# Differential attention and its gated product in one unrolled block, with each head's scores directly behind its v projection

## The chip, the cores and the metric

The kernel runs on one core of a Trainium2 chip. The metric is device time in microseconds (us), from one execution's start to its end; three executions of the kernel before were timed, and one further execution was profiled. TensorE (PE), VectorE (DVE), ScalarE (ACT), GpSimd (POOL) and SyncE (SP, which issues the DMA) each run their own instructions strictly in the order written, and wait for one another through semaphores.

## What is computed

Two transformer layers in fp32 for 512 tokens and model width 1024. The change is in the second layer, in the differential attention branch and its gate:

```python
h = _rmsnorm(x, mix_pre_g)
q, k, v, z, xbc, dt_raw, gate_logits = jnp.split(h @ w_in, cuts, axis=-1)
p = probs(q1b, k1) - lam * probs(q2b, k2)          # causal softmax, two maps a head, 8 heads
o = _rmsnorm(p @ v, da_subln_g, SUBLN_EPS) * (1.0 - lam_init)
attn_out = o @ w_branch_attn
dt = jax.nn.softplus(dt_raw + ssd_dt_bias)         # cumulative sums of -exp(A_log) * dt feed the SSD branch
g_attn, g_ssd = jnp.split(jax.nn.sigmoid(gate_logits + b_gate), N_BRANCH, axis=-1)
mixed = (g_attn * attn_out + g_ssd * ssd_out) @ w_mix_out
```

The kernel keeps activations transposed (features on partitions, tokens in the free dimension). Heads are 128 wide, so one head's q, k or v is one tile of 128 features by 512 tokens.

## The kernel before

Everything that is a matrix product with weights is done in **units**. A unit is a 128x1024 piece of weights that SP loads into one of two raw buffers (`c.raw`); ACT rounds it to `w_hi` (L155, `split_hi`), DVE subtracts to get `w_lo` (L166, `split_lo`), and PE then issues 24 matmuls of 128x512 (L193 to L195, `multiply_tile`) into one of two PSUM banks (`acc`). Buffers alternate by the unit's number, so unit k+2 is split into the buffers that unit k leaves. `split_hi(k)` therefore waits until PE has used unit k, and `split_lo(k)` for that `split_hi`. An accumulator bank is free again when its reader has taken it (`acc_free`), and the tile two later may start.

The attention is `da_stage`. For each of 8 heads PE runs the units q, k and v; ACT copies the three tiles out of the banks (L1842). A head further has: `turn_v` (v to token-major by four transposes into the bank `mixed`, L1805); `scores` (two maps by four row blocks of 128, 256, 384 and 512 columns, in two banks in turn, L1273); `maxima` (DVE reads each score tile out of its bank with the mask added and the row maximum, L1287, which frees the bank for the tile after next); `exponentials` (ACT, eight of them, L1299); `weights` (DVE: reciprocal and the difference of the two maps, L1909 to L1922); `transposes` of the probabilities on PE (L1308), each block taken out by ACT (`take_transposes`, L1316) from one of two banks; `outputs` (L1327); and the norm of the output: square (ACT L1851), its sum over the features by a matmul with ones (`mixed`, L1830), root (ACT L1855 and L1857), product (DVE L1927), and the hi/lo split (ACT L1861, DVE L1932).

A head's second half (transposes, outputs, norm) is done one head later, among the units of the next head. PE's order in one head is q unit, `turn_v` of the head one back, k unit, `transposes` of the head one back, `scores` of this head, `outputs` of the head one back, v unit, sum of squares of the head one back. The loop over heads is a device loop (`Fori`) of three rounds with two heads each; the first head and the last are written out.

Then come a barrier, a block in which GpSimd clears the semaphores (`clear_semaphores`, L247), and `gated_stage`: eight rounds of one gate unit (`h` times the gate's weights, sigmoid on ACT, L1694) and one value unit (the attention's output times `w_branch_attn`), whose product DVE forms (L1726) straight from the bank. Between its rounds it runs the small steps of the SSD branch (`SsdSteps`): `project` (24 matmuls), `argument`, `exponentials`, `logarithm`, `steps` (a chain of DVE operations on 32x512 up to a scan, L2204 to L2212), `turn` (transposes of the sums), `tables`. The next stage, `ssd_stage`, begins behind another barrier.

## Time and profile before

| | |
|---|---|
| median of 3 executions | 2933.54 us (2932.46 to 2940.70) |
| the profiled execution: its own time | 2936.5 us |
| its span, first to last instruction | 2934.5 us |
| PE busy | 2687.7 us, 92% of the span |
| DVE, ACT busy | 1291.6 us (44%), 1051.4 us (36%) |
| mean granted PE clock | 0.958 of 2.4 GHz |

How to read it: the span is what the instructions cover; the execution's own time is 2.0 us longer. A matmul's busy time is modelled and overlaps its neighbours, so positions in time are taken from the starts of rows: the distance from the start of a piece of PE work to the start of the next piece is what the piece costs on PE. A row of the timeline is a start, a duration, the engine, the line, what is written and read, and a count; in brackets stand the idle time in front of it and who ended that. A row of busy time by stretch gives start and end, its length, then busy time and count of PE, of PE's weight loads, of DVE, ACT and POOL, the granted PE clock (1.00 is 2.4 GHz, 0.50 is 1.2 GHz), the DMA share and GB/s.

### The profile page before, as it was taken

Reading aid. Unit: us, or ns where it says so; the run is one execution under the profiler, and the core shown is the slowest. Engines: PE = TensorE matmul, PEld = TensorE weight load, DVE = VectorE, ACT = ScalarE, POOL = GpSimd, SP = SyncE. Lnnn points to the kernel's source line nnn. Section 1 sums busy time; section 2 is a strip of 40 time slices with the busy share of each in tenths; the row PEclk is TensorE's granted clock in tenths of the full one; section 3 lists DMA queues with packets and bytes.
Section 4 is the critical chain, followed back from the end, with each engine's and each line's share of the span. In section 5 each row is a group of like instructions: output and inputs, shape, how many; then the busy total and the mean of one; then the engine's idle time right before and its main releaser. Section 6 shows DMA issues by size and latency. Waiting matters only on the chain. (4 is left out here: it accounts for less than half of the span.)

```text
span 2934.5 us, 34310 instructions
## 1 busy us (share of the span) xinstructions
PE 2687.7 (92%) x12052; PEld 2161.0 (74%) x12052; DVE 1291.6 (44%) x1765; ACT 1051.4 (36%) x1661; POOL 180.4 (6%) x111
## 2 busy tenths in 40 slices
PE   4998999999999999996999898988799798799997
PEld 3777777788888888884676677766677587588885
DVE  5343544344443444424343236666634633533333
ACT  4343544243222323223344334444522433323221
POOL 0000000010001000012000000011202300100000
PEclk8999999999999999997898899999999899899998
DMA  2212121222223323331111122232122131122232
GB/s 88 66 64 74 59 70 60 91 93 93 100 91 99 97 95 98 97 94 51 58 50 50 63 92 96 82 107 93 64 93 100 65 101 65 58 94 99 94 97 81
DMA packets 69457, 241.00 MB, mean 82 GB/s; under 512 B 7968, under 2 KB 8992, under 8 KB 69264
## 3 DMA queue, kind: packets, MB, share of 16 engines
q1 hardware_dynamic: 69392, 240.14, 25.2%
q8 instruction: 40, 0.66, 0.1%
q14 instruction: 25, 0.20, 0.0%
HBM read 237.94 MB, written 2.16 MB: 82 GB/s over the span
## 5 line engine op out<-in xcount | busy, mean ns | idle before, releaser
L193 PE MATMUL acc<-h_hi,w_hi 128*128 128x512 f32 x2176 | 873.8, 402 | 47.7 <-PEq L227 18.5
L166 DVE TENSOR_TENSOR w_lo<-w_raw,w_hi 128x1024 fp32r<-128x1024 f32 (+1 forms) x422 | 513.9, 1218 | 824.2 <-ACT w_hi L155 823.6
L194 PE MATMUL acc<-h_lo,w_hi 128*128 128x512 f32 x2176 | 854.7, 393 | 0.0
L195 PE MATMUL acc<-h_hi,w_lo 128*128 128x512 f32 x2176 | 854.3, 393 | 0.0
L155 ACT ACTIVATE w_hi<-w_raw 128x1024 fp32r<-128x1024 f32 (+1 forms) x422 | 441.5, 1046 | 1138.1 <-PE acc L195 1135.8
L193 PEld LDWEIGHTS acc<-h_hi,w_hi 128*128 128x128 f32 x2176 | 413.5, 190 | 148.3 <-issue 58.5
L194 PEld LDWEIGHTS acc<-h_lo,w_hi 128*128 128x128 f32 x2176 | 413.5, 190 | 90.4 <-issue 6.4
L195 PEld LDWEIGHTS acc<-h_hi,w_lo 128*128 128x128 f32 x2176 | 413.0, 190 | 87.8
L193 PE MATMUL acc<-9_hid_hi,w_hi 128*128 128x512 f32 x352 | 136.9, 389 | 0.0
L194 PE MATMUL acc<-9_hid_lo,w_hi 128*128 128x512 f32 x352 | 136.9, 389 | 0.0
L195 PE MATMUL acc<-9_hid_hi,w_lo 128*128 128x512 f32 x352 | 136.9, 389 | 0.0
L613 POOL TENSOR_TENSOR ssq<-ssq,10_sq 128x512 f32<-128x512 f32 x24 | 42.4, 1766 | 1275.7 <-ACT 10_sq L602 1275.7
L756 DVE TENSOR_TENSOR 9_up<-acc,10_rstd 128x512 f32<-128x512 f32 x44 | 30.4, 691 | 128.7 <-PE acc L195 128.7
L751 DVE TENSOR_TENSOR 9_gate<-acc,10_rstd 128x512 f32<-128x512 f32 x44 | 30.4, 691 | 105.8 <-PE acc L195 96.0
L194 PEld LDWEIGHTS acc<-9_hid_lo,w_hi 128*128 128x128 f32 x352 | 66.1, 188 | 13.8
L195 PEld LDWEIGHTS acc<-9_hid_hi,w_lo 128*128 128x128 f32 x352 | 66.1, 188 | 13.7
L193 PEld LDWEIGHTS acc<-9_hid_hi,w_hi 128*128 128x128 f32 x352 | 66.1, 188 | 13.7
L193 PE MATMUL acc<-29_hid_hi,w_hi 128*128 128x512 f32 x176 | 68.5, 389 | 0.0
L194 PE MATMUL acc<-29_hid_lo,w_hi 128*128 128x512 f32 x176 | 68.5, 389 | 0.0
L195 PE MATMUL acc<-29_hid_hi,w_lo 128*128 128x512 f32 x176 | 68.5, 389 | 0.0
L193 PE MATMUL acc<-merged_hi,w_hi 128*128 128x512 f32 x128 | 52.2, 407 | 11.8 <-PEq L227 6.1
L2490 POOL TENSOR_TENSOR 17_xs<-17_xs,17_moved 128x384 f32<-128x384 f32 x16 | 18.5, 1155 | 683.6 <-DVE 17_xs L2473 683.0
(427 smaller groups left out, 3438.2 us busy)
## 6 DMA issues: line engine op xcount, KB each, us to landing
w_raw<-in_w_gu SPq DMA_DIRECT2D x132, 512.0 KB, 3.4
w_raw<-in_w_down SPq DMA_DIRECT2D x48, 512.0 KB, 3.5
w_raw<-in_w_ssd SPq DMA_DIRECT2D x40, 512.0 KB, 3.4
w_raw<-in_w_swa SPq DMA_DIRECT2D x28, 512.0 KB, 3.4
w_raw<-in_w_gla SPq DMA_DIRECT2D x24, 512.0 KB, 3.4
w_raw<-in_w_da SPq DMA_DIRECT2D x24, 512.0 KB, 3.4
w_raw<-in_w_ssd_out SPq DMA_DIRECT2D x24, 512.0 KB, 3.4
w_raw<-in_w_xa SPq DMA_DIRECT2D x24, 512.0 KB, 3.4
```

The source lines that it names most:

```text
L155: c.nc.scalar.activation(c.w_hi[:, k % 2, 0:chunks * P], c.raw[:, k % 2, 0:chunks * P], ACT.Copy).then_inc(c.hi_done, 1)
L166: c.nc.vector.tensor_tensor(c.w_lo[:, k % 2, 0:chunks * P], c.raw[:, k % 2, 0:chunks * P], c.w_hi[:, k % 2, 0:chunks * P].bitcast(F32), AL ...
L193: pe.matmul(out, hi, x_hi[:, j, 0:cols], start=first, stop=False)
L194: pe.matmul(out, hi, x_lo[:, j, 0:cols], start=False, stop=False)
L195: mm = pe.matmul(out, lo, x_hi[:, j, 0:cols], start=False, stop=final)
L613: pool.tensor_tensor(self.c.ssq[:], self.c.ssq[:], self.sq[:, par, :], ALU.add).then_inc(self.summed, 1)
L751: dve.tensor_tensor(gate[:], c.acc[0][:], root.rstd[:], ALU.mult).then_inc(gate_done, 1)
L756: dve.tensor_tensor(up[:], c.acc[1][:], root.rstd[:], ALU.mult).then_inc(c.acc_free[1], 1)
L2490: pool.tensor_tensor(y[:, j, P:], y[:, j, P:], moved[:, j % 2, P:], ALU.add).then_inc(q["joined"], 1)
```

## The change

`da_stage` and the attention's `gated_stage` become one stage, `branch_stage`, with no device loop. All 40 units stand in one list: for heads 0 to 5 q, k, v and the gate unit with the head's number; for heads 6 and 7 q, k and v; then gate units 6 and 7 and the eight value units. On PE a head's `scores` stand behind its v unit, and `outputs` and the sum of squares of the head one back directly behind the scores, ahead of the gate unit. ACT and DVE get orders of their own, written out: ACT splits the k unit's weights ahead of `take_transposes`, and writes each gate's sigmoid straight into the result buffer `part_attn`, with a load of the sigmoid's table ahead and of the exponential's table behind. DVE splits the weights for q, k and v and then runs `maxima`. The steps of the SSD branch stand at fixed places: `project` and `transposes` of head 7 between gate units 6 and 7, `turn` behind value unit 3, the last matmul (`last_rows`) behind value unit 4. They take the banks and buffers of scores, q and k, which are idle by then. `clear_semaphores` runs ahead of this block and once more ahead of the last feed-forward, instead of in the middle. The number of matmuls is the same.

```diff
--- before.py
+++ after.py
@@ class Norm
-        self.rstd, self.normed = sb("rstd", [P, S]), sb("normed", [P, NORM_BUFS, S])
+        if places is None:
+            normed = sb("normed", [P, NORM_BUFS, S])
+            places = [normed[:, n, :] for n in range(NORM_BUFS)]
...
@@ gated_stage
-        rounds_with(pe, body, *([None, steps.project, None, steps.turn] if steps else []))
+        rounds_of(c, pe, body)
...
@@ class SsdSteps
-        self.proj, self.turned, self.whole = ps("proj"), [ps("turned0"), ps("turned1")], ps("whole")
+        self.proj, *self.turned, self.whole = banks
...
+    def last_rows(self, pe):
+        H = SSD_HEADS
         pe.wait_ge(self.tok_done, 1)
         pe.matmul(self.whole[:, 0:NT * H], self.last[:], self.by_tok[:], start=True, stop=True).then_inc(self.whole_done, 1)
@@ new
+def branch_units(a):
+    order = [(n, g) for g in range(DA_HEADS - 2) for n in ("q", "k", "v", "gate")]
+    order += [(n, g) for g in (DA_HEADS - 2, DA_HEADS - 1) for n in ("q", "k", "v")]
+    order += [("gate", DA_HEADS - 2), ("gate", DA_HEADS - 1)] + [("value", g) for g in range(KC)]
...
+@stage
+def branch_stage(c, ctx, places, y_hi, y_lo, causal, gain, part, steps):
...
+    @block.sync
+    def _(sp):
+        sp.dma_start(mask[:], causal).then_inc(tables_in, 16)
+        steps.load(sp)
+        n = c.stream.n
+        for k in range(n):
+            ahead, u = (c.stream, k + 2) if k + 2 < n else (c.following, k + 2 - n)
+            chunks, src = ahead.units[u]
+            if k == places["value", KC - 2]:
+                steps.store(sp)
+            sp.wait_ge(c.lo_done, c.unit + k + 1)
+            load_unit(c, sp, k % 2, chunks, src(0))
+        sp.wait_ge(steps.stored, 16)
...
+        def turn_v(g):
+            wait_evacuated(c, pe, 0, places["v", g])
+            pe.wait_ge(mixed_free, 2 * g + 1)
+            for n in range(NT):
+                mm = pe.transpose(mixed[:, n * P:(n + 1) * P], v[:, g % 2, n * P:(n + 1) * P], c.ident[:])
+            mm.then_inc(v_turned, 1)
...
+        def mean_square(g):
+            pe.wait_ge(squared, g + 1)
+            pe.wait_ge(mixed_free, 2 * g + 2)
+            pe.matmul(mixed[:], c.ones[:], sq[:], start=True, stop=True).then_inc(total, 1)
...
+        unit(0, "q")
+        unit(0, "k")
+        unit(0, "v")
+        score(0)
+        unit(0, "gate")
+        turn_v(0)
+        for g in range(1, H):
+            unit(g, "q")
+            unit(g, "k")
+            att.transposes(pe, g - 1, (g - 1) % 2)
+            unit(g, "v")
+            score(g)
+            outputs(g - 1)
+            mean_square(g - 1)
+            if g not in LATE:
+                unit(g, "gate")
+            if g < H - 1:
+                turn_v(g)
+        unit(H - 2, "gate")
+        turn_v(H - 1)
+        pe.wait_ge(att.read, H * att.n + 2)
+        steps.project(pe)
+        att.transposes(pe, H - 1, (H - 1) % 2)
+        unit(H - 1, "gate")
+        outputs(H - 1)
+        mean_square(H - 1)
+        for j in range(4):
+            value(j)
+        pe.wait_ge(att.pt_done, att.turns + H * NT)
+        steps.turn(pe)
+        value(4)
+        steps.last_rows(pe)
+        for j in range(5, KC):
+            value(j)
...
+        def square(g):
+            act.wait_ge(att.outs, g + 2)
+            act.activation(sq[:], att.out[0][:], ACT.Square).then_inc(squared, 1)
...
+        def gate(g):
+            k = places["gate", g]
+            weights_hi(g, "gate")
+            act.preload_act_table(ACT.Sigmoid)
+            bias = c.small[:, SMALL["b_gate_2"][0] + g:SMALL["b_gate_2"][0] + g + 1]
+            act.activation(part[:, g, :], c.acc[k % 2][:], ACT.Sigmoid, bias=bias).then_inc(c.acc_free[k % 2], 1)
+            act.preload_act_table_set(EXP_LN_SET)
...
+        for g in range(H):
+            take(g, "q", q)
+            weights_hi(g, "q")
+            take(g, "k", k_)
+            weights_hi(g, "k")
+            if g > 0:
+                att.take_transposes(act, g - 1)
+            take(g, "v", v)
+            weights_hi(g, "v")
+            if g > 0:
+                square(g - 1)
+            att.exponentials(act, g, g % 2)
+            if g > 0:
+                roots(g - 1)
+                y_split(g - 1)
+            if g == 4:
+                steps.split_weights(act)
+            if g not in LATE:
+                gate(g)
+            if g < H - 1:
+                take_v_tok(g)
+        gate(H - 2)
+        take_v_tok(H - 1)
+        steps.exponentials(act)
+        att.take_transposes(act, H - 1)
+        gate(H - 1)
+        square(H - 1)
+        roots(H - 1)
+        y_split(H - 1)
+        for j in range(2):
+            weights_hi(j, "value")
+        steps.logarithm(act)
+        for j in range(2, 5):
+            weights_hi(j, "value")
+        steps.tables(act)
+        for j in range(5, KC):
+            weights_hi(j, "value")
...
+        def product(j):
+            k = places["value", j]
+            wait_evacuated(c, dve, 0, places["gate", j])
+            wait_tile(c, dve, 0, k)
+            dve.tensor_tensor(part[:, j, :], part[:, j, :], c.acc[k % 2][:], ALU.mult).then_inc(c.acc_free[k % 2], 1)
+            weights_lo(j, "value")
+        for g in range(H):
+            weights_lo(g, "q")
+            weights_lo(g, "k")
+            weights_lo(g, "v")
+            att.maxima(dve, g, g % 2)
+            if g == H - 2:
+                weights(g)
+            if g > 0:
+                normed_output(g - 1)
+            if g == 4:
+                steps.split_weights_lo(dve)
+            if g not in LATE:
+                weights_lo(g, "gate")
+            if g == H - 1:
+                y_split(g - 1)
+                weights_lo(H - 2, "gate")
+            if g != H - 2:
+                weights(g)
+            if 0 < g < H - 1:
+                y_split(g - 1)
+        steps.argument(dve)
+        weights_lo(H - 1, "gate")
+        normed_output(H - 1)
+        y_split(H - 1)
+        for j in range(2):
+            product(j)
+        steps.steps(dve)
+        for j in range(2, 5):
+            product(j)
+        steps.to_end(dve)
+        for j in range(5, KC):
+            product(j)
@@ build_program
         with ExitStack() as f:
...
+        clear_semaphores(c)
...
-                da_stage(c, s_da, s_att, *y_da, a["causal"], "mix_pre_g_2")
-                clear_semaphores(c)
-                gated_stage(c, s_att, s_ssd, [[y_da]], 1, None, None, None, part, 0,
-                            (tok, scratch, a["w_dt"], a["keep"], a["last"]))
+                branch_stage(c, s_da, s_ssd, branch_places, *y_da, a["causal"], "mix_pre_g_2", part,
+                             (tok, scratch, a["w_dt"], a["keep"], a["last"]))
...
+        clear_semaphores(c)
         with ExitStack() as f:
```

In the order of instructions, on DVE in the scores of the first head: the last weight split before the scores' reads, and what follows (`w_lo` is a unit's low part, `13_score` the two score banks, `12_mask` the causal mask, `13_s` the scores in SBUF; ISA rows on a score are the reads of `maxima`). The kernel before:

```order
L166 TENSOR_TENSOR w_lo<-w_raw,w_hi 128x1024
L1287 ISA 13_s_0,13_top<-13_score,12_mask 128x128
L1287 ISA 13_top 128x1
L1287 ISA 13_s_1,13_top<-13_score,12_mask 128x128
L1287 ISA 13_top 128x1
```

The change:

```order
L166 TENSOR_TENSOR w_lo<-w_raw,w_hi 128x1024 x3
L1291 ISA 13_s_0,13_top<-13_score,12_mask 128x128
L1291 ISA 13_top 128x1
L1291 ISA 13_s_1,13_top<-13_score,12_mask 128x128
L1291 ISA 13_top 128x1
```

Before, one weight split (that of q's slot) stands ahead of the reads and the others behind; now all three (q, k, v) stand ahead, in every head.

On ACT, around the k unit of a head with a head behind it (`12_k` is k, `13_turn` the banks of the transposed probabilities, `13_pt` their copy, `13_out` the output's bank). The kernel before:

```order
L1842 ACTIVATE 12_k<-acc 128x512
L1314 ISA
L1316 ACTIVATE 13_pt<-13_turn 128x128
L1314 REGISTER_ALU
L1316 ACTIVATE 13_pt<-13_turn 128x256
L1314 REGISTER_ALU
L1316 ACTIVATE 13_pt<-13_turn 128x384
L1314 REGISTER_ALU
L1316 ACTIVATE 13_pt<-13_turn 128x512
L154 ISA
L155 ACTIVATE w_hi<-w_raw 128x1024
```

The change:

```order
L2145 ACTIVATE 12_k<-acc 128x512
L155 ACTIVATE w_hi<-w_raw 128x1024
L1320 ACTIVATE 13_pt<-13_turn 128x128
L1320 ACTIVATE 13_pt<-13_turn 128x256
L1320 ACTIVATE 13_pt<-13_turn 128x384
L1320 ACTIVATE 13_pt<-13_turn 128x512
L2145 ACTIVATE 12_v<-acc 128x512
L155 ACTIVATE w_hi<-w_raw 128x1024
L2155 ACTIVATE 12_sq<-13_out 128x512
```

The weight split of k's slot has moved from behind the four copies of transposed probabilities to ahead of them.

On PE, behind the scores of a head (`12_mixed` with `12_sq` is the sum of squares). The kernel before:

```order
L1273 MATMUL 13_score<-12_k,12_q 128x512
L1321 ISA
L1327 MATMUL 13_out<-13_pt,12_v_tok 128x128 x10
L186 REGISTER_ALU
L193 MATMUL acc<-h_hi,w_hi 128x512
```

The change:

```order
L1277 MATMUL 13_score<-12_k,12_q 128x512 x2
L1331 MATMUL 13_out<-13_pt,12_v_tok 128x128 x10
L2097 MATMUL 12_mixed<-12_sq,ones 128x512
L193 MATMUL acc<-h_hi,w_hi 128x512
```

Before, the v unit's 24 matmuls stood between the outputs and the sum of squares; now nothing does, and the gate unit follows the sum.

## Rows read from the trace of the kernel before

**Rows 1.** Busy time by stretch: head 6, the seam, the gated stage twice

```profile
1569.50:1600.20 30.70, 28.63 (x126) 22.00 (x125) 12.34 (x33) 13.51 (x31) 0.00 (x0) 0.89 0.16 49
1624.60:1646.90 22.30, 9.42 (x39) 6.89 (x37) 7.29 (x14) 8.65 (x15) 0.00 (x0) 0.68 0.00 0
1646.90:1693.50 46.60, 46.56 (x192) 38.31 (x193) 11.60 (x11) 11.47 (x13) 0.00 (x0) 0.93 0.35 115
1693.50:1731.60 38.10, 38.10 (x169) 31.35 (x167) 15.12 (x15) 15.32 (x17) 0.00 (x0) 1.00 0.21 70
```

**Rows 2.** Timeline of PE in one steady head, most of the weight units left out

```profile
1544.67 0.49 PE L1308 MATMUL 13_turn<-ident,13_s 128*128 128x128 f32 x3
...
1546.66 0.49 PE L1273 MATMUL 13_score<-12_k,12_q 64*128 64x128 f32 x4
...
1553.27 4.54 PE L1327 MATMUL 13_out<-13_pt,12_v_tok 128*128 128x128 f32 x20
...
1557.56 0.49 PE L193 MATMUL acc<-h_hi,w_hi 128*128 128x512 f32 x1
...
1563.14 1.02 PE L1830 MATMUL 12_mixed<-12_sq,ones 128*128 128x512 f32 x2
...
1564.24 0.39 PE L194 MATMUL acc<-h_lo,w_hi 128*128 128x512 f32 x1
```

**Rows 3.** Timeline of ACT in the same head

```profile
1540.70 1.06 ACT L155 ACTIVATE w_hi<-w_raw 128x1024 fp32r<-128x1024 f32 x1
1544.87 0.60 ACT L1842 ACTIVATE 12_k<-acc 128x512 f32<-128x512 f32 x1 [3.11 <-PE acc L195]
1545.36 0.55 ACT L1316 ACTIVATE 13_pt<-13_turn 128x128 f32<-128x128 f32 x2
...
1557.85 0.60 ACT L1851 ACTIVATE 12_sq<-13_out 128x512 f32<-128x512 f32 x1 [9.54 <-PE 13_out L1327]
1558.34 0.39 ACT L1299 ACTIVATE 13_s<-13_s,13_ntop 128x128 f32<-128x128 f32 x1
```

**Rows 4.** Timeline of DVE in the same head

```profile
1541.79 1.23 DVE L166 TENSOR_TENSOR w_lo<-w_raw,w_hi 128x1024 fp32r<-128x1024 f32 x1 [2.42 <-ACT w_hi L155]
1547.34 0.29 DVE L1287 CUSTOM_DVE_ANT_0 13_s<-13_score,12_mask 128x128 f32<-128x128 f32 x1 [4.32 <-PE 13_score L1273]
...
1562.84 0.20 DVE L1909 RECIPROCAL 13_rec<-13_den 128x8 f32<-128x8 f32 x1 [7.12 <-ACT 13_s L1299]
...
1566.54 1.23 DVE L166 TENSOR_TENSOR w_lo<-w_raw,w_hi 128x1024 fp32r<-128x1024 f32 x1
1567.68 0.74 DVE L1927 SCALAR_TENSOR_TENSOR 12_y<-13_out,small,12_rstd 128x512 f32<-128x512 f32 x1
```

**Rows 5.** Busy time by stretch: scores and outputs; behind the turn's pause

```profile
1427.90:1434.70 6.80, 6.39 (x22) 4.89 (x23) 3.47 (x10) 0.00 (x0) 0.00 (x0) 0.50 0.07 11
1734.90:1747.60 12.70, 12.70 (x49) 9.99 (x48) 3.06 (x4) 3.63 (x7) 0.00 (x0) 0.87 0.27 89
```

**Rows 6.** Timeline of PE at the seam and at the gated stage's end

```profile
1624.56 1.02 PE L1830 MATMUL 12_mixed<-12_sq,ones 128*128 128x512 f32 x2
...
1639.96 1.13 PE L1830 MATMUL 12_mixed<-12_sq,ones 128*128 128x512 f32 x2 [0.69 <-ACT 12_sq L1851]
1646.94 0.79 PE L193 MATMUL acc<-h_hi,w_hi 128*128 128x512 f32 x1 [5.86 <-PEq L247]
...
1751.53 0.49 PE L193 MATMUL acc<-h_hi,w_hi 128*128 128x512 f32 x1 [3.93 <-PEq L227]
```

**Rows 7.** Timeline of ACT behind a table load

```profile
1725.31 1.28 ACT L1705 ACT_TABLE_LOAD   x1
1726.61 1.06 ACT L155 ACTIVATE w_hi<-w_raw 128x1024 fp32r<-128x1024 f32 x1
```

**Rows 8.** Timeline of DVE: start and end of the chain of SSD steps

```profile
1724.21 0.41 DVE L2204 TENSOR_SCALAR 16_u<-16_e 32x512 f32<-32x512 f32 x1 [0.39 <-DVEq L1738]
...
1733.48 2.36 DVE L166 TENSOR_TENSOR w_lo<-w_raw,w_hi 128x1024 fp32r<-128x1024 f32 x2
```

More of the change, by code:

```diff
@@ L356, in on_vector @@
                     dve.wait_ge(self.lo_done[last % 2], last // 2 + 1)
-                dve.scalar_tensor_tensor(self.normed[:, k % NORM_BUFS, :], self.c.x[:, k, :], vec(self.c, self.gain, k),
+                dve.scalar_tensor_tensor(self.places[k % NORM_BUFS], self.c.x[:, k, :], vec(self.c, self.gain, k),
                                          self.rstd[:], ALU.mult, ALU.mult).then_inc(self.normed_done, 1)
@@ L1623, in gated_stage @@
 @stage
-def gated_stage(c, ctx, branches, per, prior, out_hi, out_lo, out, gate_bias=None, steps=None, whole=None):
+def gated_stage(c, ctx, branches, per, prior, out_hi, out_lo, out, gate_bias=None, whole=None):
     sb, ps, sem = local(c, ctx)
@@ L1633, in gated_stage @@
     units = [1 + len(parts) for parts in branches]
-    steps = SsdSteps(c, ctx, *steps) if steps else None
     block = ctx.enter_context(c.nc.Block())
     split = Split(c, ctx, *whole) if whole is not None else None
-    def rounds_with(eng, body, *beside):
-        if steps is None:
-            return rounds_of(c, eng, body)
-        n = c.stream.rounds
-        cuts = (0, n // 4, n // 2, 3 * n // 4, n - 1)
-        for part, (first, end) in zip(beside, zip(cuts, cuts[1:])):
-            with eng.Fori(first, end) as i:
-                body(i, False)
-            if part is not None:
-                part(eng)
-        body(n - 1, c.following is None)
     def tiles():
@@ L1661, in _ @@
     def _(sp):
-        if steps is not None:
-            steps.load(sp)
         stream_loads(c, sp, c.stream, c.following)
-        if steps is not None:
-            steps.store(sp)
     @block.gpsimd
@@ L1700, in body @@
                                    ACT.Copy).then_inc(hi_done, 1)
-        def then_sigmoid(part):
-            def run(act):
-                part(act)
-                act.preload_act_table(ACT.Sigmoid)
-            return run
-        rounds_with(act, body, *([steps.split_weights, then_sigmoid(steps.exponentials), then_sigmoid(steps.logarithm),
-                                  then_sigmoid(steps.tables)] if steps else []))
+        rounds_of(c, act, body)
     @block.vector
@@ L1745, in body @@
                         dve.wait_ge(lo_done, per * i + t + 1)
[L1746 removed]
+        rounds_of(c, dve, body)
 LAM_INIT = 0.2
[L1753 to L1946 removed]
@@ L2099, with __init__ @@
 class SsdSteps:
-    def __init__(self, c, ctx, tok, scratch, w_dt, keep_in, last_in):
+    def __init__(self, c, ctx, tok, scratch, w_dt, keep_in, last_in, banks, places):
         H = SSD_HEADS
@@ L2160, in exponentials @@
         act.wait_ge(self.dve_done, 1)
-        act.activation(self.e[:], self.x[:], ACT.Abs).then_inc(self.act_done, 1)
+        act.activation(self.e, self.x, ACT.Abs).then_inc(self.act_done, 1)
         act.wait_ge(self.act_done, 2)
-        act.activation(self.e[:], self.e[:], ACT.Exp, scale=-1.0).then_inc(self.act_done, 1)
+        act.activation(self.e, self.e, ACT.Exp, scale=-1.0).then_inc(self.act_done, 1)
     def logarithm(self, act):
@@ L2167, in logarithm @@
         act.wait_ge(self.dve_done, 2)
-        act.activation(self.v[:], self.u[:], ACT.Ln).then_inc(self.act_done, 1)
+        act.activation(self.v, self.u, ACT.Ln).then_inc(self.act_done, 1)
     def tables(self, act):
@@ L2209, in steps @@
         self._step(dve, dve.tensor_tensor(v, v, e, ALU.add))
-        self._step(dve, dve.scalar_tensor_tensor(self.dt[:], self.x[:], 0.0, v, ALU.max, ALU.add))
+        self._step(dve, dve.scalar_tensor_tensor(self.dt[:], self.x, 0.0, v, ALU.max, ALU.add))
         self._step(dve, dve.tensor_scalar(u, self.dt[:], self.a_neg[:], -1.0, ALU.mult, ALU.mult))
@@ L2217, in to_end, with source @@
                                           self.tok[:, :, SUM], ALU.subtract))
+def branch_units(a):
+    order = [(n, g) for g in range(DA_HEADS - 2) for n in ("q", "k", "v", "gate")]
+    order += [(n, g) for g in (DA_HEADS - 2, DA_HEADS - 1) for n in ("q", "k", "v")]
+    order += [("gate", DA_HEADS - 2), ("gate", DA_HEADS - 1)] + [("value", g) for g in range(KC)]
+    def source(n, g):
+        if n in ("gate", "value"):
+            return a["w_attn_2"][g, 0 if n == "gate" else 1]
+        return a["w_da"][g // 2, 3 * (g % 2) + ("q", "k", "v").index(n)]
+    return ([(KC, lambda i, n=n, g=g: source(n, g)) for n, g in order],
+            {u: k for k, u in enumerate(order)})
@@ L2521, in build_program @@
     s_dn2 = down("w_down1_2")
-    s_da = Stream(DA_HEADS // 2, [whole("w_da", u) for u in range(6)], 6)
-    s_att = Stream(KC, [whole("w_attn_2", u) for u in range(2)], 2)
+    units, branch_places = branch_units(a)
+    s_da = Stream(1, units, len(units))
     s_ssd = Stream(SSD_GROUPS, [whole("w_ssd", u) for u in range(10)], 10)
```

300 lines of the change are left out of this document (124 added, 176 removed).

## The prediction

> **What bounds the kernel now.** PE is busy for 92% of the span, so I read PE's row first and ask where it stands still or runs at half clock. I compared stretches of the two stages that the change joins. In the gated stage there is nothing to gain inside the rounds: PE is busy for 46.56 of 46.60 us and 38.10 of 38.10 us [rows 1]. One unit of 24 matmuls costs 24/168 of 38.1, which is 5.44 us. A steady head takes 30.7 us [rows 1] for three units (16.3 us) and 14.4 us of attention work. The seam between the stages takes 22.3 us with PE busy for 9.42, at 0.68 of the clock [rows 1]; exactly, from the sum of squares at 1624.56 to the first gate matmul at 1646.94, 22.4 us [rows 6]. That seam is what the joined block can give back.
>
> Then I looked at how a head's pieces hand over, since the change rewrites these handovers in every head. The timeline of PE shows scores from 1546.66 to 1553.27, outputs to 1557.56, then the v unit to 1563.14, and the sum of squares with no pause before it [rows 2]. Scores are paced by DVE: two banks, and DVE's first read starts 0.68 us after the first score matmul [rows 2, 4]. The square is done long before PE wants it, since the v unit lies between. In a score phase the granted clock falls: 6.8 us at 0.50 in a head, over the last scores and the outputs [rows 5]; at 6.39 busy that costs some 3.2 us a head already.
>
> **The change, priced.** Let T be the end of a head's v unit on PE.
>
> (a) Scores wait for v's weight split. DVE now has all three splits ahead of `maxima`, and the third hangs on v. The first two scores fill both banks at once; then PE stands until DVE reads. From T: ACT starts its copy 0.20 later (as 1544.67 to 1544.87), the next ACT row starts 0.49 later (1544.87 to 1545.36), the low part on DVE starts 1.09 behind the start of the high part (1540.70 to 1541.79), and the next DVE row 1.14 behind that (1566.54 to 1567.68) [rows 2, 3, 4]. Sum 2.92 us, against 0.68 now: 2.24 us. From the first read on, the scores take as long as before (1547.34 to 1553.27, 5.93 us). Queued behind it on PE are outputs and the gate unit; nothing else covers it. Eight heads: +17.9.
>
> (b) Transposes wait for k's weight split. Only two banks take them, so PE stops after the second block until ACT copies. That copy stands 0.69 us behind the k unit now (0.20 and 0.49) and has one split more ahead of it, about 1.0 us (a row of 1.06, [rows 3]). PE had no slack there. Seven heads: +7.0. The last head's is in (f).
>
> (c) The sum of squares waits for the square. The square starts 0.29 us behind the outputs (1557.56 to 1557.85), takes 0.60 and hands over in some 0.05; the same handover showed an idle 0.69 at the seam [rows 2, 3, 6]. 0.94 us in each of seven heads: +6.6.
>
> (d) Head 6 has no gate unit. `turn_v` needs the bank `mixed`, which is free when ACT has read the sum of squares, and ACT does that only behind the eight exponentials of this head. From the end of the outputs: 0.29 + 0.49 for the square, 4.50 for exponentials (1558.34 to 1562.84), 0.72 for the logarithm: 6.0 us. PE is there after 0.94 + 0.87 (the sum of squares, 1563.14 to 1564.24 less one matmul of 0.23), 1.8 us [rows 2, 3, 4]. A stall of 4.2 us. In heads 1 to 5 the gate unit's 5.44 us cover it, with 1.2 us to spare. Behind such a pause the clock is low for a while: 48 weight matmuls took 12.6 of the 12.70 us at 0.87 instead of 10.9, 1.7 us [rows 5]. Together +5.9.
>
> (e) With the pause in front, part of the 6.8 us of low clock now lies in idle time, and the outputs (4.29 us at half clock, half of that at full) run partly fast. Between 0 and 2.1 us; no row tells where the low stretch will begin, so I take 0.8 in seven heads: -5.6.
>
> (f) The tail. Before, beyond its units: the seam 22.4, then 46.6 for 192 matmuls that need 43.5, so 3.1 lost to the low clock, then 3.3 for the turn (1731.60 to 1734.90) and 1.7 for the clock behind it: 30.4 us [rows 1, 5, 6]. Now: `turn_v` 0.4. Transposes of head 7 need ACT, which stands in the SSD exponentials behind `project` (argument, two activations and handovers, then the copies): 4.5 from `project` to the next unit. Then gate unit 7; behind it ACT does a split, two table loads of 1.3 (1725.31 to 1726.61, [rows 7]) and the sigmoid, 4.4 in all, before the square, then 0.65 and the sum of squares 0.87: 5.9. The DVE chain of 9.3 us (1724.21 to 1733.48, [rows 8]) starts 2.5 behind value unit 1, as now beside the split; three units of 16.3 cover it but the split for value unit 4 waits: 2.5 with the turn. `last_rows` needs ACT behind a split and a table load: 3.3. Three pauses with 1.7 of low clock each: 5.1. Sum 21.7, so -8.7.
>
> (g) A clear of the semaphores more than before outside the seam, twice. With one, PE idled 5.86, at the next stage end without one 3.93 [rows 6]: at most 1.9 each, at least nothing. I take 1.0: +2.0 in all.
>
> Costed at nothing: the gates' extra table loads in heads 0 to 5. ACT has the sigmoid done some 11.4 us behind the outputs, and the bank is wanted for the next k unit at 12.9; if that cover were gone, each 1 us late would cost 1 us in six heads. SP's three loads for the SSD steps now stand before the weight stream; the queue's next weights are wanted a unit (5.44 us) later. The weight loads and matmuls are the same in number. The branches of the device loop go, but over the loop turns in the gated stage PE idles for 0.04 us [rows 1], so nothing comes back.
>
> The Trainium skill speaks here: "ScalarE: Activation LUTs", What ACT_TABLE_LOAD costs, gives about 1.28 us for the load and another 1.38 us of drain for every switch. The trace shows the load at 1.28 us and the next row 1.30 us after its start, so no drain [rows 7]. By the page, six loads on the tail's path would add 8.3 us, and the sum would be 33 instead of 25.
>
> **Sum:** 17.9 + 7.0 + 6.6 + 5.9 - 5.6 - 8.7 + 2.0 = +25.1 us. On the profiled execution's own 2936.5 that is 2961.6. That execution stood 3.0 above the median, so around the median 2933.5 the same sum gives 2958.6. I write 2958.
>
> **Rivals.**
>
> 1. The clock falls further. PE idles in a second place of each head (0.94 at the square) and longer at the scores; if a second stretch like that of 6.8 us [rows 5] follows, over the gate unit, seven heads pay 3.2 more, and (e) vanishes: +25 + 22 + 6 = +53 at the worst, 2987; half of that, 2972, if it comes in some heads. For it: at the turn a pause of about 2 us was enough for a low stretch. Against: the heads now recover under one weight unit. The Trainium skill ("TensorE: Matmul & The Clock Gate", A second HAM failure mode) says that frequent short idle times between groups make the clock swing; the trace agrees for the scores.
>
> 2. The joined tail gives nothing: each of its handovers costs what the old seam cost, -8.7 becomes 0, 2967. For it: five waits on ACT in it. Against: PE has units of work between them.
>
> 3. Not slower, by the clock. If the new pause takes in the whole low stretch, each head is 3.2 us better, instead of 0.8 in seven (-16.8 more, and -3.2 in head 0), and the low clock behind the four pauses of (d) and (f) is gone (-6.8): 25.1 - 26.8 = -1.7, 2932. It decides from about 2.2 us a head. Against: the pause lies ahead of the last scores, and a low stretch has so far begun behind low activity, not in it.
>
> 4. The wait behind v does not come, since DVE is served otherwise than I read: (a) falls away, +7.2, 2941: no change that can be told. Against: DVE's row of instructions allows nothing else. Faster than before would need (b) or (c) to be hidden too: 25.1 - 17.9 - 7.0 - 6.6 = -6.4, still within the bound.
>
> **Chances.** Forecast 0.55; rival 1 0.15; rival 2 0.12; rival 3 0.07; rival 4 0.06; something outside these that makes it faster 0.05. What a measurement can tell from no change is 0.3%, 8.8 us. Slower by more: 0.82. Within: 0.12. Faster: 0.06. The range reaches from rival 4's 2941 to some low clock more, 2976. The forecast's own is 2949 to 2970: (e) between 0 and 2.1 a head, (g) between 0 and 3.9.
>
> **What would show it.** In the profile after: two score matmul pairs behind each v unit, then PE idle for about 2.3 us released by DVE's score reads; first DVE read 2.9 us behind the v unit; transposes idle 1.6 instead of 0.6; about 0.7 idle, released by the square, before each sum of squares; one idle of about 4 us before `turn_v` of head 6; a steady head with gate near 39.5 us against 30.7 + 5.4. The prediction is wrong if a head with its gate comes at or under 36.2 us, if no idle time stands at the scores' second pair, or if the tail, from the sum of squares behind head 7's scores to the end of the last value unit, takes less than 75 us or over 90 us (ten units and `project` are 59.9 of it).

## The result, and the profile after

| | before | after |
|---|---|---|
| median | 2933.72 us (2932.46 to 2940.70, 4 runs) | 2972.81 us (2970.03 to 2977.89, 4 runs) |
| ratio to before, 95% interval | | 1.0131 [1.0116, 1.0145] |
| profiled execution, its span | 2936.5, 2934.5 us | 2970.79, 2969.0 us |
| mean granted PE clock | 0.958 | 0.954 |

The changed kernel is 1.3% slower, 39 us by the medians and 34.3 us between the two profiled executions. The forecast was 2958: right in sign, inside the range of 2940 to 2976, but 15 us too low, and the time lies above the forecast's own 2949 to 2970.

PE's timeline of the kernel after, from the scores of head 4 to the first unit of the stage that follows, weight units left out (start, duration, what, and in brackets the idle time in front and who ended it):

```profile
1560.43 0.49 PE L1277 MATMUL 13_score<-12_k,12_q 64*128 64x128 f32 x4
1563.60 1.43 PE L1277 MATMUL 13_score<-12_k,12_q 64*128 64x256 f32 x4 [2.68 <-DVE 13_top L1291]
1565.49 1.99 PE L1277 MATMUL 13_score<-12_k,12_q 64*128 64x384 f32 x4 [0.46 <-DVE 13_top L1291]
1567.95 2.55 PE L1277 MATMUL 13_score<-12_k,12_q 64*128 64x512 f32 x4 [0.46 <-DVE 13_top L1291]
1570.43 4.12 PE L1331 MATMUL 13_out<-13_pt,12_v_tok 128*128 128x128 f32 x20
1575.23 1.12 PE L2097 MATMUL 12_mixed<-12_sq,ones 128*128 128x512 f32 x2 [0.69 <-ACT 12_sq L2155]
...
1657.20 1.12 PE L2097 MATMUL 12_mixed<-12_sq,ones 128*128 128x512 f32 x2 [0.69 <-ACT 12_sq L2155]
1662.21 0.74 PE L2082 MATMUL 12_mixed<-ident,12_v 128*128 128x128 f32 x4 [3.89 <-ACT 12_rstd L2159]
1662.60 0.78 PE L193 MATMUL acc<-h_hi,w_hi 128*128 128x512 f32 x1
...
1675.19 0.49 PE L1312 MATMUL 13_turn<-ident,13_s 128*128 128x128 f32 x3
1677.24 0.96 PE L1312 MATMUL 13_turn<-ident,13_s 128*128 128x128 f32 x7 [1.56 <-ACT 13_pt L1320]
...
1698.26 1.13 PE L2097 MATMUL 12_mixed<-12_sq,ones 128*128 128x512 f32 x2 [0.69 <-ACT 12_sq L2155]
...
1713.34 1.30 PE L1312 MATMUL 13_turn<-ident,13_s 128*128 128x128 f32 x7 [2.10 <-ACT 13_pt L1320]
...
1726.45 1.13 PE L2097 MATMUL 12_mixed<-12_sq,ones 128*128 128x512 f32 x2 [2.82 <-ACT 12_sq L2155]
...
1753.48 0.47 PE L193 MATMUL acc<-y_da_hi,w_hi 128*128 128x512 f32 x1 [1.20 <-DVE w_lo L166]
...
1763.53 0.49 PE L1934 MATMUL 13_turn<-15_by_tok,15_last 128*128 128x128 f32 x2 [2.74 <-ACT 15_by_tok L1958]
...
1781.62 0.39 PE L195 MATMUL acc<-y_da_hi,w_lo 128*128 128x512 f32 x1
1785.01 0.49 PE L193 MATMUL acc<-h_hi,w_hi 128*128 128x512 f32 x1 [3.01 <-PEq L227]
```

The kernel before, from the transposes to the second score pair of the same head:

```profile
1515.08 0.95 PE L1308 MATMUL 13_turn<-ident,13_s 128*128 128x128 f32 x7 [0.62 <-ACT 13_pt L1316]
1515.96 0.49 PE L1273 MATMUL 13_score<-12_k,12_q 64*128 64x128 f32 x4
1516.99 0.93 PE L1273 MATMUL 13_score<-12_k,12_q 64*128 64x256 f32 x4 [0.54 <-DVE 13_top L1287]
```

Every pause that the prediction named is there: 2.68 us before the second score pair, 1.56 in the transposes, 0.69 before each sum of squares, 3.89 before `turn_v` of head 6. The last row stood at 1751.53 before [rows 6], so 33.5 of the 34.5 us of span have come by the end of the joined block; 0.4 of them stand ahead of its first unit (1383.27 before, 1383.66 after).

DVE's timeline at the same scores says who is late:

```profile
1562.11 1.23 DVE L166 TENSOR_TENSOR w_lo<-w_raw,w_hi 128x1024 fp32r<-128x1024 f32 x1 [7.09 <-ACT w_hi L155]
1563.25 0.28 DVE L1291 CUSTOM_DVE_ANT_0 13_s<-13_score,12_mask 128x128 f32<-128x128 f32 x1
```

DVE had been idle for 7.09 us, waiting for v's high part, before it could split and then read the first scores, which had been in their bank since about 1560.9. DVE is 44% busy in this kernel, yet its order alone holds PE up.

One thing the prediction had wrong shows in the durations. The same score pairs took 0.93 and 1.25 us before; in this head the 256-column pair takes 1.43 and the 384-column pair 1.99. The busy time by stretch gives the granted clock (the last number but two), first for the whole head, then around the scores:

```profile
1541.00:1582.00 41.00, 35.15 (x150) 26.48 (x149) 13.45 (x33) 17.67 (x36) 0.00 (x0) 0.88 0.16 52
1563.40:1564.40 1.00, 0.80 (x4) 0.71 (x4) 0.35 (x4) 0.00 (x0) 0.00 (x0) 0.60 0.16 33
1564.40:1573.40 9.00, 8.07 (x25) 4.79 (x23) 3.31 (x13) 0.00 (x0) 0.00 (x0) 0.50 0.17 55
1573.40:1574.40 1.00, 1.00 (x8) 0.95 (x7) 0.00 (x0) 0.00 (x0) 0.00 (x0) 0.78 0.00 0
```

The clock stands at its lower level, 1.2 GHz, from just behind the pause almost to the end of the outputs, 10.2 us by the clock records, against 6.8 us before [rows 5]. Six of the eight heads (0 and 3 to 7) have a stretch of 10.2 us. Heads 1 and 2 have one of 6.8; it begins 1.1 and 2.4 us behind the second pair's start, though their pause is the same 2.68 us.

### The profile page after: what moved, and what is told of

Its sections match the earlier page's. It is cut to its first block and busy times, and to the rows that moved or that the text cites. A ratio compares the mean times of both kernels' runs of the same rounds, so it can differ in the third digit from the quotient of the medians.

```text
span 2969.0 us, 33820 instructions
## 1 busy us (share of the span) xinstructions
PE 2695.5 (91%) x12052; PEld 2162.3 (73%) x12052; DVE 1293.2 (44%) x1765; ACT 1062.4 (36%) x1669; POOL 180.6 (6%) x111
## 5 line engine op out<-in xcount | busy, mean ns | idle before, releaser
L1277 PE MATMUL 13_score<-12_k,12_q 64*128 64x128 f32 (+3 forms) x128 | 49.8, 738 | 28.5 <-DVE 13_top L1291 28.5
L193 PE MATMUL acc<-28_hid_hi,w_hi 128*128 128x512 f32 x176 | 68.5, 389 | 0.0
L194 PE MATMUL acc<-28_hid_lo,w_hi 128*128 128x512 f32 x176 | 68.5, 389 | 0.0
L195 PE MATMUL acc<-28_hid_hi,w_lo 128*128 128x512 f32 x176 | 68.5, 389 | 0.0
L193 PE MATMUL acc<-merged_hi,w_hi 128*128 128x512 f32 x128 | 51.7, 404 | 11.9 <-PEq L227 6.1
```

The costliest lines, as they stand in the source:

```text
L193: pe.matmul(out, hi, x_hi[:, j, 0:cols], start=first, stop=False)
L194: pe.matmul(out, hi, x_lo[:, j, 0:cols], start=False, stop=False)
L195: mm = pe.matmul(out, lo, x_hi[:, j, 0:cols], start=False, stop=final)
L1277: mm = pe.matmul(self.score[j % 2][:, 0:count * P], q[:, n * P:(n + 1) * P], k[:, first * P:(first + count) * P], start=a == 0, stop=a == ...
```

## The experiments

The two theories. **Sum of waits:** the loss is what PE's idle times in the heads show, each set by the place of one instruction on ACT or DVE, with a clock surcharge behind the pause at the scores. **Place of the scores:** what costs is that scores, outputs and the sum of squares now stand together behind v, whatever ACT and DVE do. e1, e2 and e3 each undo one thing, e4 fills one pause. Differences below are between medians. The kernel before was timed again beside the runs, with medians of 2933.0 (e1, e2, e4, e6), 2934.8 (e0, e3, e5, e8) and 2935.5 us (e7, e9, e10), so where two runs have different neighbours, the difference of their ratios is the better measure.

**e1: DVE reads the scores ahead of v's split.**

```diff
             weights_lo(g, "k")
-            weights_lo(g, "v")
             att.maxima(dve, g, g % 2)
+            weights_lo(g, "v")
```

> The change, with one thing altered: DVE runs the score reads of a head ahead of the split of v's weights instead of behind it. Theory (a wait behind v's weight split is the largest loss): the first read starts some 0.7 us behind the first score matmul instead of 2.9, the idle time before the second score pair falls from 2.68 to about 0.5 us, and eight heads give back 8 x 2.1 = 17 us; if the longer low clock was caused by that pause, up to 2 us more in each of five heads, 27 us in all. So 2946 to 2956 against 2973 for the change. Rival (the time is lost to the joined block as such, code and clock, not to this wait): less than 8 us come back, 2965 or more.

Measured: 2940.76 us (2932.93 to 2947.92), ratio to before 1.0022 [1.0011, 1.0034]. That is 32.1 us less than the change. PE's timeline of this kernel:

```profile
1550.50 0.49 PE L1277 MATMUL 13_score<-12_k,12_q 64*128 64x128 f32 x4
1551.53 0.93 PE L1277 MATMUL 13_score<-12_k,12_q 64*128 64x256 f32 x4 [0.53 <-DVE 13_top L1291]
1552.90 1.55 PE L1277 MATMUL 13_score<-12_k,12_q 64*128 64x384 f32 x4 [0.44 <-DVE 13_top L1291]
1554.62 2.71 PE L1277 MATMUL 13_score<-12_k,12_q 64*128 64x512 f32 x4 [0.17 <-DVE 13_top L1291]
1557.26 4.05 PE L1331 MATMUL 13_out<-13_pt,12_v_tok 128*128 128x128 f32 x20
```

The idle time before the second pair is 2.15 us shorter, 17.2 in eight heads. The low clock now begins in the third pair and lasts 6.8 us, in seven heads, with none in the last. Between the profiled executions the block ends 28.9 us earlier: 17.2 of idle time, and the remaining 11.7 is put down to the clock (the block has 65.5 us of low clock instead of 98.5). So the place of one instruction cost more than its own idle time, and more than was expected of it: the time is below the 2946 to 2956 on record.

**e2: ACT copies the transposes ahead of k's split.**

```diff
-            weights_hi(g, "k")
             if g > 0:
                 att.take_transposes(act, g - 1)
+            weights_hi(g, "k")
```

> The change, with ACT copying the transposed probabilities ahead of the split of k's weights. Theory: the idle time inside the transposes falls from 1.56 to 0.6 us in seven heads, 6.6 us in all: about 2966 against 2973. Rival (the v unit or the scores behind it wait for something else anyway, so that the idle time only moves): no change within 2 us.

Measured: 2959.37 us (2958.93 to 2966.46), ratio 1.0100 [1.0085, 1.0115], 13.4 less than the change. The profile has the idle time of before:

```profile
1551.99 0.95 PE L1312 MATMUL 13_turn<-ident,13_s 128*128 128x128 f32 x7 [0.62 <-ACT 13_pt L1320]
```

The pause shrank by 0.94 us a head, 6.6 in seven. The two ratios put the gain at 9 us, the medians at 13.4; between the profiled executions the block is 11.9 us shorter (389.99 instead of 401.86). Part of what goes beyond the 6.6 is clock: four heads have a stretch of 10.2 us here and four one of 6.8, against six and two, and two heads with the shorter one are 1.5 us shorter from the first score to the end of the outputs.

**e3: the sum of squares behind the gate unit** (and `turn_v` behind the next q unit, since it needs the same bank).

```diff
             outputs(g - 1)
-            mean_square(g - 1)
             if g not in LATE:
                 unit(g, "gate")
-            if g < H - 1:
-                turn_v(g)
+            mean_square(g - 1)
```

> The change, with the sum of squares of the head one back moved on PE from directly behind the outputs to behind the gate unit, and the turn of v (with ACT's copy of it) from ahead of the next q unit to behind it. Theory: the wait for the square (0.94 us) is covered in the five heads that have a gate unit and an output, 4.7 us, and the stall of 3.9 us ahead of head 6's turn of v with its slower unit behind (1.7) is gone, 5.6 us: 10 us in all, some 2962. Rival (these handovers only move a wait to the next bank or weight split): within 3 us of the change.

Measured: 2960.28 us (2953.14 to 2966.61), ratio 1.0085 [1.0072, 1.0098], 12.5 less. The idle time at the square is gone in the five heads that have a gate unit to cover it (it stays in the last two), and so is the stall of head 6. In one of the heads a new pause stands ahead of the k unit:

```profile
1583.96 0.60 PE L2082 MATMUL 12_mixed<-ident,12_v 128*128 128x128 f32 x4
1585.51 0.50 PE L193 MATMUL acc<-h_hi,w_hi 128*128 128x512 f32 x1 [0.94 <-ACT part_attn L2173]
```

The k unit waits for the bank of head 4's gate unit, which ACT frees with the sigmoid. ACT's timeline just before:

```profile
1581.46 1.04 ACT L1939 ACTIVATE 15_hi<-15_raw 128x1024 fp32r<-128x1024 f32 x1
...
1583.47 1.28 ACT L2171 ACT_TABLE_LOAD   x1
1584.77 0.69 ACT L2173 ACTIVATE part_attn<-acc,small 128x512 f32<-128x512 f32 x1
```

This is the cover that the prediction costed at nothing ("ACT has the sigmoid done some 11.4 us behind the outputs, and the bank is wanted for the next k unit at 12.9"). It held in every head of the change, and holds in four of the five here. Head 4 is the one in which ACT also splits the weights of the SSD steps (`15_hi`, 0.95 us to the next row) ahead of the gate's split, and there the slack is used up. The k unit is also due earlier by the pause that went, and ACT's root waits for a later sum; these were not tried apart.

**e4: PE kept busy in the pause.** Ten matmuls whose result is overwritten stand ahead of each head's scores; they are extra work.

```diff
+            pe.wait_ge(att.read, g * att.n + 1)
+            for _ in range(10):
+                pe.matmul(att.score[0][:], c.h_hi[:, 0, 0:P], c.h_hi[:, 1, :], start=True, stop=True)
             att.scores(pe, g, lambda m: [(q[64 * m:64 * m + 64, g % 2, :], k_[64 * m:64 * m + 64, g % 2, :])])
```

> The change, with ten matmuls of 128x512 (2.3 us at full clock) added ahead of each head's scores; they write a score bank that the scores then overwrite, so PE does work in the pause that it has anyway. All waits stay. Theory (the pause in the scores makes the low-clock stretch begin earlier and last longer): the added work costs nothing by itself, the low stretch begins later, the second and third score pairs run at full clock, and 1 to 2.5 us a head come back, 8 to 20 us in all: 2953 to 2965. Rival (the low clock has nothing to do with the pause): the low stretches stay at 10.2 us in five heads and the time is the change's, 2973, or up to 3 us more for the second bank's first matmul.

Measured: 2963.53 us (2962.14 to 2964.01), ratio 1.0107 [1.0092, 1.0123], 9.3 less than the change, with more work. PE's timeline:

```profile
1556.42 2.43 PE L2090 MATMUL 13_score<-h_hi 128*128 128x512 f32 x10
1558.78 0.49 PE L1277 MATMUL 13_score<-12_k,12_q 64*128 64x128 f32 x4
1559.80 0.93 PE L1277 MATMUL 13_score<-12_k,12_q 64*128 64x256 f32 x4 [0.53 <-DVE 13_top L1291]
1561.18 1.25 PE L1277 MATMUL 13_score<-12_k,12_q 64*128 64x384 f32 x4 [0.45 <-DVE 13_top L1291]
```

The second pair comes 3.38 us after PE could have begun the scores, against 3.17 in the change: the wait is no shorter. But the pairs take 0.93 and 1.25 us, and the low stretches are 3.4 or 6.8 us long. This isolates the clock: idleness in the pause, not the delay as such, costs about 9 of the 32 us (7 by the ratios), near the 11.7 that e1's profile leaves to it.

**e0: the change once more**, to see how far the clock stretches are a trait of the kernel.

> The change itself once more, beside the next three kernels. Expected: 2970 to 2978, a ratio to before within 1.0116 to 1.0145. If its profile again has low-clock stretches of 10.2 us in most heads, that is a trait of the kernel; if it has 6.8 everywhere, the longer stretches were one execution's.

Measured: 2973.98 us (2969.46 to 2976.00), ratio 1.0129 [1.0114, 1.0144]. Here seven heads have 10.2 us of low clock and one (head 0) has 6.8, so the long stretches are a trait of the kernel, but not their number.

**e5: the edits of e1, e2 and e3 together.** Scores and outputs still stand behind v, ahead of the gate unit.

> The change with all three handovers mended at once: score reads ahead of v's split, transposed copies ahead of k's split, sum of squares behind the gate unit and turn of v behind the next q. Theory (the three costs are separate and add): e1 gave 32, e2 9 to 13, the third is expected at 10, so 2973 - 52 = 2921, between 2915 and 2927, at or below the old order in the joined block (2919 measured). Rival (the placing of the scores behind v is itself the loss): it stays 8 us or more above the old order, 2927 or more.

Measured: 2918.88 us (2917.62 to 2930.82), ratio 0.9949 [0.9936, 0.9962]. The three single gains are 32.1, 13.4 and 12.5, 58.0 in all; together they give 53.9. They add up but for 4 us (by the ratios 55 against 53).

**e6: the order of before inside the heads, in the joined block.** All three engines (only PE's edit is shown).

```diff
-            unit(g, "v")
             score(g)
             outputs(g - 1)
+            unit(g, "v")
             mean_square(g - 1)
```

> The joined, unrolled block of the change with the kernel before's order inside a head: scores behind the transposes and ahead of v, v between outputs and sum of squares, the turn of v behind the next q, ACT and DVE in the order of before; the gate unit behind the sum of squares, the tail as in the change. Theory (the joining is worth 8.7 us in the tail and costs 1 to 2 us for the second clear, and the order inside the head costs the rest): a head with its gate takes 36.2 us, 2926 to 2932, a little faster than before's 2934. Rival (the joined block itself costs, through its tail or its clock): 2940 or more.

Measured: 2918.97 us (2910.54 to 2920.99), ratio 0.9957 [0.9943, 0.9971]. It was expected at 2926 to 2932, with 36.2 us a head, and is below that. It is e5's time to 0.1 us (2 us by the ratios). So the place of the scores costs nothing that can be told, which here means less than some 5 us; the splits ahead of the reads and copies, the place of the sum of squares, and the stall of head 6 were the whole loss. The profiles bear it out: a head at full clock takes 33.4 us in e5 (sums of squares at 1453.51 and 1486.94) and 33.2 here. The joined block by itself is a gain of about 14 us over the kernel before (8 to 17 by the interval of the ratio). Two neighbouring heads of this kernel, by stretch:

```profile
1492.30:1525.50 33.20, 31.14 (x150) 24.12 (x149) 13.55 (x33) 17.94 (x35) 0.00 (x0) 1.00 0.20 64
1525.50:1561.60 36.10, 34.03 (x150) 26.48 (x149) 14.69 (x34) 18.78 (x36) 0.00 (x0) 0.91 0.17 54
```

The same 150 matmuls take 33.2 us at full clock and 36.1 with one low stretch. In this execution, the fastest of its kernel, three heads have a low stretch at their scores; before, all eight had.

**e8: the wait put into the old order.** Against e6, DVE reads the scores behind k's split instead of ahead of it.

```diff
-            att.maxima(dve, g, g % 2)
             weights_lo(g, "k")
+            att.maxima(dve, g, g % 2)
             weights(g)
```

> The joined block with the old order in a head (2919 us), with one thing altered: DVE splits k's weights ahead of the score reads. That puts the same pause of about 2.2 us ahead of DVE's first read, now with the scores behind k and no other handover of the change present. Theory (the pause is the change's main loss, wherever the scores stand): eight pauses cost 17.6 us, and the low-clock stretches grow again by as much as e1 gained beyond its 17 us, 10 to 15 us: 2937 to 2952. Rival (the pause costs only its own length): 2934 to 2938. Second rival (in the change the pause cost much because the scores stood behind v): under 2930.

Measured: 2942.94 us (2941.36 to 2945.45), ratio 1.0031 [1.0020, 1.0042], 24.0 more than e6. PE's timeline:

```profile
1548.83 0.96 PE L1277 MATMUL 13_score<-12_k,12_q 64*128 64x256 f32 x4 [2.68 <-DVE 13_top L1291]
1550.20 1.99 PE L1277 MATMUL 13_score<-12_k,12_q 64*128 64x384 f32 x4 [0.41 <-DVE 13_top L1291]
```

The same 2.68 us, in another order, behind another unit: 2.15 more in each of seven heads and 1.4 in the first is 16.4. The other 5 to 8 us (the ratios put the loss at 22) go with the clock: all eight heads have a low stretch at their scores, against three in the profile of e6. One split ahead of the reads makes the loss, wherever the scores stand. But six of the stretches last 6.8 us and only those of heads 0 and 7 last 10.2, so the pause alone does not make a stretch the long one.

**e7: `turn_v` of head 6 behind the q unit of head 7** (and ACT's copy of it behind q's).

```diff
             unit(g, "q")
+            if g == H - 1:
+                turn_v(g - 1)
             unit(g, "k")
```

> The change with one edit: for head 6, which has no gate unit behind its sum of squares, turn_v stands behind the q unit of head 7 on PE, and its copy behind q's copy on ACT. By the prediction's step (d) the idle time of 3.89 us at 1662.21 was PE waiting for ACT to finish head 6's exponentials, and 1.7 us more of low clock followed: both should go, so 5.6 us less than the change, near 2967, and a q unit of head 7 that starts at once behind the sum of squares. A rival: the q unit itself waits for something at that place (its accumulator bank or its low part), and then the pause only moves, with under 2 us gained. A second rival: the clock stays low in the q unit anyway, since head 6's scores are as before, and only 3.9 us come back.

Measured: 2966.21 us (2963.95 to 2971.03), ratio 1.0109 [1.0094, 1.0125], 6.6 less. PE's timeline:

```profile
1657.29 1.12 PE L2097 MATMUL 12_mixed<-12_sq,ones 128*128 128x512 f32 x2 [0.69 <-ACT 12_sq L2157]
1663.71 0.60 PE L2082 MATMUL 12_mixed<-ident,12_v 128*128 128x128 f32 x4
1669.64 0.49 PE L1312 MATMUL 13_turn<-ident,13_s 128*128 128x128 f32 x3
```

From the sum of squares to the transposes it is 12.35 us, against 17.99 (1657.20 to 1675.19) in the change: 5.64, the 3.9 of idle time and the 1.7 of clock.

**e9 and e10: the tail's two pauses**, on e6 and on e5 (one edit, shown for both; `gate` gets a flag that leaves out its own weight split, not shown).

```diff
-        steps.exponentials(act)
         att.take_transposes(act, H - 1)
-        gate(H - 1)
+        steps.exponentials(act)
+        weights_hi(H - 1, "gate")
         square(H - 1)
+        gate(H - 1, split=False)
```

> The joined block with the old order inside the heads (2918.97), and two edits in the tail: ACT takes the transposed probabilities of head 7 out of their banks ahead of the exponentials of the SSD branch, and splits gate 7's weights and squares head 7's output ahead of the table load and the sigmoid. The idle times of 2.1 us in the transposes and 2.8 us ahead of the last sum of squares should both shrink to under 1 us: 3 to 4 us less, 2915. The rival is that these waits lie beside another one (the DVE chain of SSD steps, which the value units wait for anyway), which then grows by as much: within 1 us of 2919. Third: the SSD chain now starts later because its exponentials do, and costs 1 to 3 us more than it gives.

> The three edits together (score reads ahead of v's weight split, copies ahead of k's, the sum of squares behind the gate unit; 2918.88) with the same two edits in the tail. If the tail's waits are worth what they show, 3 to 4 us less: 2915, as with the old order. If scores behind v cost nothing of their own, this and the old order with the tail's edits agree within 3 us; if one of them is over 5 us apart, the place of the scores has a price that the additive account leaves out. The rival for the tail as before: within 1 us of 2919.

Measured: e9 2915.20 us (2908.95 to 2917.78), ratio 0.9925 [0.9912, 0.9939]; e10 2915.96 us (2911.89 to 2922.29), ratio 0.9927 [0.9913, 0.9940]. That is 3.8 and 2.9 us less than e6 and e5 (9 and 6 by the ratios). PE's timeline of e9:

```profile
1662.16 0.95 PE L1312 MATMUL 13_turn<-ident,13_s 128*128 128x128 f32 x7 [0.30 <-ACT 13_pt L1320]
...
1671.51 1.12 PE L2097 MATMUL 12_mixed<-12_sq,ones 128*128 128x512 f32 x2 [0.69 <-ACT 12_sq L2153]
...
1678.41 0.50 PE L193 MATMUL acc<-y_da_hi,w_hi 128*128 128x512 f32 x1 [0.97 <-DVE y_da_lo L2268]
```

The idle times fell from 2.07 and 2.83 us in e6 to 0.30 and 0.69, 3.9 us together. A new one of 0.97 stands ahead of the first value unit, which e6 did not have; the waits behind it are as they were. From the first score of head 7 to the first unit of the next stage it is 94.16 us against 98.49 in e6 (1635.55 to 1729.71, 1630.31 to 1728.80), 4.3 less; the part beyond the idle times goes with a low stretch of 3.4 us that e6 has at its last sum of squares and e9 has not. The two orders are again less than 1 us apart. These are the fastest versions tried, some 20 us (0.75%) under the kernel before.

## Why the prediction was right, and where it was not

By the prediction's own terms, in us, each measured between the two profiled executions:

| term | predicted | measured | from |
|---|---|---|---|
| (a) scores behind v's split | +17.9 | +17.1 | (3.17 - 1.03) x 8, first score to second pair |
| (b) transposes behind k's split | +7.0 | +6.6 | (1.56 - 0.62) x 7 |
| (c) sum of squares behind the square | +6.6 | +6.6 | 0.94 x 7, end of the outputs (0.29 ahead of the square) to the sum |
| (d) `turn_v` of head 6 | +5.9 | +5.6 | 3.9 idle; 12.6 for 48 matmuls instead of 10.9 |
| (e) clock at scores and outputs | -5.6 | +3.9 | what is left of the block's 33.1 |
| (f) tail | -8.7 | -6.7 | 83.6 from 1698.26 to the last value unit's end, 81.6 predicted |
| (g) two clears | +2.0 | +1.4 | 0.4 ahead of the block, 1.0 of span behind it |
| sum | +25.1 | +34.5 | |

**(a) to (d)** were right within 1 us each, and each was then undone alone: in the profiles of e1, e2 and e7 the idle time that the change added is gone, and in e3 in the five heads where a gate unit can cover it. e8 made (a) anew in another place.

**(e) is the step that failed.** It said that "part of the 6.8 us of low clock now lies in idle time", between 0 and 2.1 us, a gain of 0.8 a head. In six heads the low stretch does not lie in the pause: the granted clock is 1.00 in the us before 1563.40, and falls directly behind the pause, for longer than before. In head 4 scores take 10.00 us from first to outputs (1560.43 to 1570.43) instead of 6.61 [rows 2], 1.25 more than the idle time; the outputs, 3.86 us to their end instead of 4.29, give back 0.43. So 0.8 us is lost where 0.8 was to be gained. Read in the same way, heads 3 to 7 lose 0.7 to 0.9 each, heads 1 and 2 gain 0.4 and 0.2, and head 0, for which nothing was counted, loses 1.0: +4.4 in all. The table's +3.9 is a remainder, and also holds what no term names, such as the wait of the next stage's first unit, 3.01 us instead of 3.93. Heads with their gate came at 39.7, 39.9, 41.0, 41.0 and 41.0 us, where 39.5 was forecast. The bound itself was at fault: the prediction weighed how much of a given low stretch the pause could hide, and never that the pause could go with a longer one. The row for it was there: the slow matmuls behind the turn's pause [rows 5], which it used for (d) and (f) but not here.

**The bounds.** The forecast's own 2949 to 2970 does not follow from its terms: with (e) between 0 and 2.1 us a head and (g) between 0 and 3.9, the same sum gives 2948 to 2966. And the upper end of the whole range, 2976, is "some low clock more" and has no sum behind it, so that it is in part luck that 2973 lies inside.

**(f)** had the right pieces: 2.8 before the sum of squares, 2.1 in the transposes, 1.2 before value unit 4, 2.7 before `last_rows`. It was 2 us too hopeful. e9 shows that its two pauses on ACT were a matter of order, all but the 0.97 us that came back.

**What was costed at nothing.** The gates' table loads stayed hidden in the change. In e3 their cover was short by 0.94 us in head 4, the one with the extra split. ACT's timeline of the kernel after shows them in the tail:

```profile
1722.50 1.28 ACT L2173 ACT_TABLE_LOAD   x1
1723.80 0.69 ACT L2175 ACTIVATE part_attn<-acc,small 128x512 f32<-128x512 f32 x1
1724.50 1.28 ACT L2176 ACT_TABLE_LOAD   x1
1725.80 0.60 ACT L2155 ACTIVATE 12_sq<-13_out 128x512 f32<-128x512 f32 x1
```

Each load takes 1.28 us and the next row starts 1.30 us after the load's start. The Trainium skill ("ScalarE: Activation LUTs", What ACT_TABLE_LOAD costs) adds some 1.38 us of drain to every switch; this trace does not agree with that part.

**Rivals.** Rival 1 gave about the right time, 2972, by a mechanism that did not come: a second low stretch over the gate unit. The granted clock is back at 1.00 in the us behind the outputs, and there is one stretch a head, in six of them a longer one. What did come of this rival is that (e)'s gain vanished. Rival 2 fell (-6.7 in the tail is not nothing), and so did 3 and 4: the clock gave nothing, and the 2.68 us stood at every second pair.

**What stays open.** How many heads of a joined block have a low stretch differs between kernels and, it seems, between executions: e6's profiled execution, 2910.54, is the fastest of its runs, e5's, 2930.82, the slowest of its own. By their clock records it is three heads against five, at some 3 us each; that is 6 us of the 20 between these two executions, and the rest was not settled. Nor was it settled what makes a stretch behind the same 2.68 us of pause last 6.8 us in one head and 10.2 in another. Nor was it settled why the same order had eight such stretches in the device loop and fewer here; so of e6's 14 us the tail's share can't be told exactly from the clock's.

## What to carry to other kernels

When work is reordered, write down for each engine what now stands ahead of the instruction that frees a buffer. Here an engine 44% busy, waiting for a weight split that nobody needed yet, held up TensorE by 2.15 us in each of eight heads; moving one line gave 32 us back. Allow for a new pause on TensorE costing more than its length: look in the trace for matmuls behind a pause of that size, and take their slower rate for what follows. Test the parts of a joined edit apart: here one part (the joined block) was worth 14 us and another (the new order inside the heads) cost 54, and the whole looked like a bad idea.

## What the runs showed that was not expected

In every head with a pause of 2.68 us at the scores (the change, e0, e2, e3, e7, e8) there is a low-clock stretch of 6.8 or 10.2 us; in heads with a pause of 0.53 it is at most 6.8, and in e5 and e6 some heads have none. Filling the pause with ten matmuls made a kernel with more work 9.3 us faster. The Trainium skill ("TensorE: Matmul & The Clock Gate", A second HAM failure mode) says that short idle times between groups of matmuls make the clock swing. The traces agree only in part: in e6 heads 1 and 2 have the same idle times at their scores (0.52, 0.44 or 0.45, and 0.47 us), one with a low stretch and one without. They put a price on it: 33.2 us against 36.1 for the same work of a head.
